# A two-layer pair of transformer and state-space blocks on one core: vector work taken out of the down projections, and the last pair's products reordered

## The reference, cut to what matters

```python
def swiglu(h, w_gate_up, w_down):
    g, u = jnp.split(h @ w_gate_up, 2, axis=-1)
    return (jax.nn.silu(g) * u) @ w_down
# odd_mixer: the decay of the recurrence
    log_a = -LRU_C * r * jax.nn.softplus(-lam)
# s5_mixer: per state decay and angle, then a scan
    decay = jnp.exp(a_re * dt)
    ab_re = decay * jnp.cos(a_im * dt); ab_im = decay * jnp.sin(a_im * dt)
    coef_re = ((nr * a_re + ni * a_im) / den)[..., None]
    y = einsum(x_re, c_re) - einsum(x_im, c_im) + d_skip * u
```

## Time and profile before

| | |
|---|---|
| time, median of 3 runs | 1730.12 us (1727.42 to 1730.45) |
| the profiled execution | 1727.55 us, span 1725.8 us, mean granted clock 0.990 |
| PE busy | 1653.2 us, 96% |
| DVE, ACT, POOL busy | 952.4, 323.9, 62.8 us |
| the chain that ended last | PE 88%, DVE 8% |
| PE's wait for weight sums in the down stages | 25.6 us in 6 waits |

### The profile page before, as it was taken

One profiled execution on the slowest core, in us unless ns is written; L12 is line 12 of the kernel. 1 busy time (PEld: TensorE's weight loads), 2 busy tenths in 40 slices (PEclk: granted clock), 3 DMA queues, 4 the chain that ended last, 5 costly groups with the idle time before them and its releaser, 6 DMA issues.

```text
span 1725.8 us, 25861 instructions
## 1 busy us (share of the span) xinstructions
PE 1653.2 (96%) x10408; PEld 1429.3 (83%) x10408; DVE 952.4 (55%) x1978; ACT 323.9 (19%) x717; POOL 62.8 (4%) x84
## 2 busy tenths in 40 slices
PE   8999999999899999999999999999997999999998
PEld 6758888889778867888898785788876988788898
DVE  6545354336666414665867476456647574434355
ACT  3241210000142102100001322322211041122200
POOL 0000000000000000193000000000000000000000
PEclk9999999999899999999999999999998999999999
DMA  6445478766454663757644233244533502445455
GB/s 229 137 132 195 145 251 302 282 227 220 159 170 148 220 233 133 248 191 245 195 171 165 80 122 98 88 145 148 158 117 116 171 27 90 140 151 154 151 171 183
DMA packets 79895, 289.42 MB, mean 168 GB/s; under 512 B 8992, under 2 KB 10016, under 8 KB 79264
## 3 DMA queue, kind: packets, MB, share of 16 engines
q1 hardware_dynamic: 79776, 287.76, 50.1%
HBM read 286.68 MB, written 1.05 MB: 167 GB/s over the span
## 4 chain that ended last, share of the span: by engine, by line
PE 88%; DVE 8%; issue 1%; ACT 1%; DMA 1%; SPq 0%; DVEq 0%; ACTq 0%
PE acc L441 54%; PE acc L572 13%; PE acc L532 4%; PE acc L1050 3%; PE acc L496 2%; PE acc L517 1%; PE acc L451 1%; PE score L1015 1%; PE acc L1029 1%; PE acc L667 1%; PE score L691 1%; PE score L647 1%; DVE probs_t L1662 1%; PE acc L990 1%; PE acc L718 1%
## 5 line engine op out<-in xcount | busy, mean ns | idle before, releaser
L441 PE MATMUL acc<-H,ring 128*128 128x256 f32 x3520 | 773.2, 381 | 13.2 <-DVE FFN L2015 3.6
L441 PEld LDWEIGHTS acc<-H,ring 128*128 128x128 f32 x3520 | 668.2, 191 | 114.6 <-issue 18.5
L441 PE MATMUL acc<-big,ring 128*128 128x256 f32 x880 | 192.1, 379 | 0.9 <-PE acc L441 0.9
L441 PEld LDWEIGHTS acc<-big,ring 128*128 128x128 f32 x880 | 166.9, 190 | 24.6 <-issue 2.0
L1855 DVE SCALAR_TENSOR_TENSOR bT<-bT,cond 128x1024 f32<-128x1024 f32 x58 | 75.2, 1297 | 79.6 <-DMA bT<-ada_in 75.8
L2056 DVE SCALAR_TENSOR_TENSOR pair<-acc,cols,pair 128x255 f32<-128x255 f32 x84 | 40.5, 483 | 119.2 <-ACT pair L1271 115.5
L1662 DVE TENSOR_TENSOR probs_t<-ring 128x512 f32<-128x512 f32 (+1 forms) x96 | 62.1, 647 | 64.5 <-PE acc L572 56.7
L572 PE MATMUL acc<-FFN,ring 128*128 128x128 f32 x760 | 93.8, 276 | 0.0
L572 PEld LDWEIGHTS acc<-FFN,ring 128*128 128x128 f32 x760 | 89.1, 192 | 0.7 <-issue 0.4
L1271 ACT ACTIVATE pair<-acc,cols 128x256 f32<-128x256 f32 x84 | 47.1, 563 | 172.5 <-PE acc L441 172.5
L1251 ACT ACTIVATE pair<-acc 128x256 f32<-128x256 f32 x42 | 16.1, 383 | 264.0 <-PE acc L441 257.5
(11 more groups left out here) (493 smaller groups left out, 1884.1 us busy)
## 6 DMA issues: line engine op xcount, KB each, us to landing
ring<-stream SPq DMA_DIRECT2D x440, 512.0 KB, 3.6
bT<-ada_in SPq DMA_DIRECT2D x70, 512.0 KB, 4.4
big<-ada_in SPq DMA_DIRECT2D x26, 512.0 KB, 4.5
big<-ssm_in SPq DMA_DIRECT2D x2, 1024.0 KB, 5.8
cols<-cols_in SPq DMA_DIRECT2D x1, 1165.5 KB, 8.8
X<-x_in SPq DMA_DIRECT2D x4, 256.0 KB, 4.9
MEM<-mem_in SPq DMA_DIRECT2D x1, 1024.0 KB, 12.0
y_out<-X SPq DMA_DIRECT2D x8, 128.0 KB, 3.5
```

The source lines that it names most:

```text
L441: mm = nc.tensor.matmul(dst, w[:, k * cols_per:(k + 1) * cols_per], r, start=first and n == 0, stop=last and n == len(src) - 1)
```

## The change

Six edits, all listed here.

1. `local_kernels` goes. GpSimd clears V and `late` (lines 1556 and 1557 of the changed kernel), ScalarE makes the eight copies after its sines of `chunk_tab`, and VectorE adds the skip gain (`skip_terms`) in `down2` after pairs j = 0, 1, 2, three, three and two at a time. TensorE waits for the copies before pair 3.
2. `lru_parameters` is split: the exponential (23 instructions) at k = 14 and the logarithm (24) at k = 16 of `up0`.
3. In `up1`: angles at k = 1 (before 2), the exponential of `state_decays` at k = 3 and the rest at k = 5 (before both 7), `input_factors` at 7 (before 8), `input_product` from 8 (before 10), all eight `drive_powers` from 14 (before from 16, the last two in `down1`). ScalarE's sines move from k = 4 to 3.
4. In pair 3 of every down stage the lone product goes into the bank `score[1]` and comes last of the last chunk; VectorE combines and updates tile 7 while it runs, then tile 6. Norms, leads and the final stores follow the order 0 to 5, 7, 6.
5. In `late_lead` the sum of squares goes to TensorE before rows 7 and 6 of the first tile.
6. `od_xb` has three lead tiles (before two).

```diff
+DOWN_ORDER = (0, 1, 2, 3, 4, 5, 7, 6)
+            return (2, 0, 1, 3) if n == 11 else (2, 3, 0, 1) if n % 3 == 2 else (0, 1, 2, 3)
...
+                        corner = score[1][:, 0:P] if j == 3 else a[:, 3 * P:4 * P]
+                        if i == 2 and j == 3:
+                            pe.wait_ge(s5_local, 8)
...
-                            if j == 0:
-                                sums(last, whole, second)
+                        elif j == 1:
+                            sums(DOWN_ORDER[-1], whole, second)
...
-            linear("od_xb", H, late_lead([("od_xb", 0), ("od_xb", 1)], gained_in_y), first=2)
+            linear("od_xb", H, late_lead([("od_xb", k) for k in range(3)], gained_in_y), first=3)
...
+            act.wait_ge(s5_cleared, 1)
+            for g, dst in enumerate((V, late)):
+                for jj in range(4):
...
+            pool.wait_ge(s5_kernels, 1)
+            own(g.memset(V, 0.0))
+            own(g.memset(late[:], 0.0))
+            pool.sem_inc(s5_cleared, 1)
...
-                    if drive:
-                        if j < 2:
-                            drive_powers(1, 2 + j, H)
-                    if name == "down0" and j == 1:
-                        lru_parameters()
...
+                    if j == 3:
+                        update(name, 7, lower_tile(b, u3_w), gain)
+                        dve.wait_ge(weight_sums_used, sum_uses(name, 11, 3))
+                        update(name, 6, upper_tile(score[1][:, 0:P], home, u3_w), gain)
...
+                    if name == "down2" and j < 3:
+                        skip_terms((3 * j, 3 * j + 1, 3 * j + 2)[0:2 if j == 2 else 3])
...
+                    if layer == 0 and k == 14:
+                        lru_exp_of()
+                    if layer == 0 and k == 16:
+                        lru_log_of()
+                    if layer == 1 and k == 1:
+                        state_angles()
```

More of the change, by code:

```diff
@@ L409, in _ @@
                     sp.dma_start(V, ssm_in[1]).then_inc(c_in, 16)
-            for k in range(KD):
-                sp.wait_ge(acc_free, 4 + TILE0["down3"] + k + 1)
+            for n, k in enumerate(DOWN_ORDER):
+                sp.wait_ge(acc_free, 4 + TILE0["down3"] + n + 1)
                 sp.dma_start(out[:, k * S:(k + 1) * S], at(X, k)).then_inc(stored, 16)
@@ L501, in lead, with late_lead @@
                 return before
-            def late_lead(tiles, src, width=S, last=KD - 1, whole=False, second=None):
+            def late_lead(tiles, src, width=S, whole=False, second=None):
                 before = outs[0]
                 outs[0] += 4
-                for js, rows in ((range(2), range(6)), (range(2), range(6, KD)), (range(2, len(tiles)), range(KD))):
+                for js, rows in ((range(2), DOWN_ORDER[0:6]), (range(2), DOWN_ORDER[6:8]), (range(2, len(tiles)), DOWN_ORDER)):
                     for j in js:
@@ L979, in _ @@
             down("down2")
-            sums(KD - 1)
+            sums(DOWN_ORDER[-1])
             def local(n):
@@ L1123, in norm @@
                 if after:
-                    for k in range(tiles):
-                        if paired and k % 2 == 0:
-                            corner(paired, k // 2)
-                        act.wait_ge(after[0], after[1] + k + 1)
+                    for n_in, k in enumerate(DOWN_ORDER if paired else range(tiles)):
+                        if paired and n_in % 2 == 0:
+                            corner(paired, n_in // 2)
+                        act.wait_ge(after[0], after[1] + n_in + 1)
                         nc.scalar.activation(at(SQ, k), at(src, k), ACT.Square).then_inc(norm_squares, 1)
@@ L1141, in double_norm @@
                 act.wait_ge(norm_sums, n)
-                for k in range(KD):
-                    if k % 2 == 0:
-                        corner("down1", k // 2)
-                    act.wait_ge(acc_free, 4 + TILE0["down1"] + k + 1)
+                for n_in, k in enumerate(DOWN_ORDER):
+                    if n_in % 2 == 0:
+                        corner("down1", n_in // 2)
+                    act.wait_ge(acc_free, 4 + TILE0["down1"] + n_in + 1)
                     nc.scalar.activation(at(M, k), at(X, k), ACT.Square, scale=col("final_norm", k))
@@ L1604, in whole_sums, with gain_tile @@
                 dve.sem_inc(norm_summed, 1)
-            def gain_tile(k, gain, dst):
+            def gain_tile(k, gain, dst, order=range(KD)):
                 if gain:
                     v.tensor_scalar(dst(k), at(X, k), gain(k), None, ALU.mult).then_inc(gained, 1)
-                if k >= 2:
-                    dve.wait_ge(norm_squares, squares[0] + k)
-                    own(v.tensor_tensor(at(SQ, 0), at(SQ, 0), at(SQ, k - 1), ALU.add))
-                if k == KD - 1:
+                n = order.index(k)
+                if n >= 2:
+                    dve.wait_ge(norm_squares, squares[0] + n)
+                    own(v.tensor_tensor(at(SQ, 0), at(SQ, 0), at(SQ, order[n - 1]), ALU.add))
+                if n == KD - 1:
                     squares[0] += KD
@@ L2108, in output_powers, with skip_terms @@
                 dve.sem_inc(s5_powers, 1)
-            def local_kernels():
-                dve.wait_ge(s5_kernels, 1)
-                own(v.memset(V, 0.0))
-                own(v.memset(late[:], 0.0))
-                for g, dst in enumerate((V, late)):
-                    for jj in range(4):
-                        rows = slice(32 * jj, 32 * jj + 32)
-                        own(v.tensor_copy(dst[rows, 0:2048].rearrange("p (n q c) -> p n q c", q=4, c=32)[:, :, jj, :],
-                                          score[g][rows, :].rearrange("p (n c) -> p n c", c=32)))
-                for i in range(KD):
+            def skip_terms(tiles):
+                dve.wait_ge(s5_local, 8)
+                for i in tiles:
                     k0 = kernels(i, 0)
```

116 lines of the change are left out of this document (68 added, 48 removed).

## The result

The changed kernel took 1691.24 us (median of 4 runs, 1690.74 to 1691.98), the kernel before beside it 1730.28: ratio 0.9778, 95% interval 0.9761 to 0.9795. The forecast was 1692.5, in a range of 1687 to 1701. The profiled execution took 1690.74 us, its span is 1689.0 (before 1725.8), the mean granted clock 0.998 (0.990). PE is busy 97% of the span; DVE 941.6 us, ACT 328.3, POOL 69.9.

What follows compares the result with a forecast made beforehand. PE was taken as the bound, busy 96% of the span, so only its waits and lower clock could yield time. Terms sum to 36.4 us: 1691.2 from 1727.55, 1693.7 from the median; forecast 1692.5, range 1687 to 1701.

Steps and rivals of the forecast that it cites:

- A: down0, pair 1: moving the softplus to up0 removes PE's 9.17 us wait and 2.5 of clock loss, 11.7 us.
- B: Behind down0: third lead tile and earlier sum of squares close the 2.44 us gap; 2.2 us taken, bounds 1.6 and 2.44.
- C: up1: spreading the parameters removes the 3.56 us wait but adds 2.5 at pair 3; net gain 1.1 us.
- D: down1: with all drive powers in up1, waits of 1.78 and 0.55 us go, 0.1 each for restart; 2.5 us.
- E: Leads behind down1: gap before dqi3 falls from 2.43 to 1.56 us, half of 1.55 clock loss returns; 1.6 us.
- F: down2: moving scan-kernel work off VectorE removes PE's 12.26 us wait and 2.85 of clock loss; 15.1 us.
- G: Behind down2: the 3.43 us chain gets about 0.67 shorter, half of 1.7 clock loss returns; 1.5 us.
- H: End of down3: the chain before the last store gets 0.67 us shorter.
- R2: Rival: the clock stays low behind gaps after down1 and down2 and the new up1 wait; 3.3 us more, 1696; chance 0.15.
- R1: Rival: GpSimd's clears slow VectorE's sums at the start of down2; 3.7 us lost, 1696; chance 0.12.
- R3: Rival: another wait right behind the removed ones, 0.97 us at nine down-stage boundaries, 8.7 us, 1701; chance 0.08.
- R4: Rival: down2's clears are so slow that the program gets slower, 1735 us at 60 us of clears; chance 0.02.

Runs made afterwards that it cites:

- e1: The changed kernel with the 47 softplus instructions back in down0, pair 1: 1702.33 us.
- e2: The changed kernel with clears, the eight copies and the eight skip gains back on VectorE ahead of down2's pairs: 1708.9 us.
- e9: The changed kernel measured once more, nothing altered: 1693.08 us.
- e10: The changed kernel with up1's angles back in pair 2 and two ada rows loaded one weight slot later: 1686.24 us.
- e8: The changed kernel with two lead tiles of od_xb in place of three: 1692.28 us.
- e4: The changed kernel with the angles of up1 back in pair 2: 1688.8 us.
- e6: The changed kernel with the sum of squares behind rows 7 and 6 of the first lead tile again: 1694.22 us.
- e7: The changed kernel with up1's parameters and two drive powers in down1 at their places of before: 1695.25 us.
- e5: The changed kernel with GpSimd's two clears written as an instruction that also reads its buffer: 1696.3 us.
- e3: The changed kernel with the lone product of pair 3 back in bank a and order 0 to 7 everywhere: 1695.21 us.

## Why the prediction was right, and where it was not

The measured 36.8 us lie close to the sum of 36.4, but closer than the parts deserve: A, B and C were together 1.5 too large, D, E, F and G 2.25 too small. That they cancel is luck.

A, F and H came within 0.2 us of their terms, and e1 and e2 show that the edits named carry A and F. H's agreement to 0.01 is luck too: from the last product to the end it is 5.9 us in the change and 5.4 in e9, the same program. The working behind F was right in its form (VectorE's sum is there just as PE comes, the corner copy is not late), and wrong by a factor of nearly two in the length of a clear: a memset of 2048 columns is 1.80 us on GpSimd, as it was 1.76 on VectorE, and not four times the 826 ns for 512. Those 826 are of a clamp to ±0.5, and a mean over unlike instructions (ns, shortest, median, longest):

```profile
L1540 POOL TENSOR_SCALAR chunk_tab<-chunk_tab x4: 612/614/1466, 786.7 to 788.8; 128x512 f32<-128x512 f32 x4
```

The one of 1466 runs beside a product of VectorE. Four times the usual 614 would have given 2.5, still too much.

D was undersized by 0.45: 2.33 us of waits and 0.6 around them, where I had added 0.2. What the 0.6 is was not looked into.

B was oversized by 0.9, and its 1.3 lies under the lower bound of 1.6. The step that failed is "The gap goes", with its allowance of 0.4 at the gates: the gap went, but PE then came to tile 7 sooner than its weights. Those stood in SyncE's queue behind an ada load that waits for a row of VectorE (SyncE's row of 478.13 under e10), and that row is done only at 478.04:

```profile
476.75 1.29 DVE L1890 SCALAR_TENSOR_TENSOR bT<-bT,cond 128x1024 f32<-128x1024 f32 x1
```

Counted from the end of down0, the weights are issued at 21.6 us in place of e8's 20.4, and PE is at tile 7 at 25.1 in place of about 26.8: both moved against each other. I had gone through VectorE and ScalarE for the cost of the third tile, not through SyncE.

C was oversized by 0.4: the new wait was 2.81 where I took 2.5 (my own terms, 723.8 less 721.2, give 2.6). e4 shows that it was avoidable.

E and G: the waits were as worked out (1.57 for 1.56, 2.76 for 2.8). For the clock I took half of 1.55 and of 1.7. In the profiled execution all of both came back, 0.8 us more in each term, which puts E at its upper bound.

R2 had a chance of 0.15 as a state of the kernel. The runs show that it is a matter of the single execution. Over the 14 profiles, the same gap in the same place:

| gap of PE | followed by the lower clock |
|---|---|
| 9.2 and 12.3 us, down0 and down2 | 4 of 4 |
| 3.15, up2 | 10 of 12 |
| 3.4 to 3.6, up1 and behind down2 | 2 of 4 |
| 2.5 to 2.8, up1 | 5 of 8 |
| 2.76, behind down2 | 4 of 11 |
| 2.43 to 2.44, od_xb and dqi3 | 1 of 3 |
| 1.57, dqi3 | 0 of 12 |

A fall behind one of the short gaps takes about 1.7 us from PE; two took about 3, e6's behind the 3.15 (0.57 over 7 us) and e7's behind 3.55 (0.59 over 7 us). So the loss in up1 that R2 named does occur, at 1.7 x 5/8 = 1.1 us on average, and the 1.7 of G is not safe. In the first measurement neither shows in the profile; in e9 the one in up1 does, and the two profiled executions lie 0.9 apart. What decides a single case stays open. I did not try to bridge the gap of 2.8 in up1.

R1 was false for this change and true for e5. R3 and R4 did not occur: but for the one wait in up1 that C foresaw and the one in od_xb under B, nothing new stands behind the old waits, and no boundary of a pair in the down stages shows a wait beyond the 0.84 and 0.89. Of the differences of 1 to 4 us between e3, e4, e6, e7, e8 and the change, only the gaps and stretches in the traces are told apart; their medians hold one or two such falls of the clock, and intervals of about 3 us either way.

## What to carry to other kernels

Cut the timelines before and after at the same events: the total hid one term of 1.1 us given back in SyncE's queue, which the table of stretches shows at once. When work is moved a step earlier to clear one wait, look one step to each side for a place with slack; here pair 2 had it and pair 1 did not. A gap of PE of 2.4 to 3.6 us here could cost more than it lasted, but not in every execution, so that a single profile neither proves nor excludes the loss: close such gaps, and judge by several executions. Idle matmuls in them are worth trying, no more than that by these runs. Before scaling a mean up, look at its shortest and longest: the mean behind F's clears mixed 0.61 and 1.47 us.

## What was not expected of the hardware

Beside a GpSimd instruction that reads and writes 128 x 2056 float32 in 1.95 us, a VectorE addition of two SBUF operands took 2.08 us in place of 0.69; beside the write-only clear of 1.81 us it took 0.69. GpSimd's clear of 2048 columns was as fast as VectorE's (1.80 against 1.76 us). Gaps of 2.4 to 3.6 us were followed by the lower clock in 22 of 38 cases, those of 1.57 ahead of dqi3 in none of 12.
